# Second feed-forward of a two-layer trunk: Strassen's seven block products in place of eight for the gate and value tiles

## The reference

```
def swiglu(h, w1, w3, w2):
    return (jax.nn.silu(h @ w1) * (h @ w3)) @ w2

x = x + mx[5] * swiglu(modulate(rmsnorm(x, norm_ffn[layer]), mx[3], mx[4]),
                       ffn_w1[layer], ffn_w3[layer], ffn_w2[layer])
```

## Time and profile before

| | |
|---|---|
| median of 3 runs | 2422.42 us (2417.39 to 2422.8) |
| profiled execution | 2426.19 us |
| span of its instructions | 2424.5 us |
| mean granted clock of TensorE | 0.976 of full speed |
| PE busy | 2308.9 us, 95% |
| POOL busy | 1043.5 us, 43% |
| DVE busy | 1402.4 us, 58% |
| ACT busy | 885.7 us, 37% |

### The profile page before, as it was taken

One profiled execution on the slowest core, in us unless ns is written; L12 is line 12 of the kernel. 1 busy time (PEld: TensorE's weight loads), 2 busy tenths in 40 slices (PEclk: granted clock), 3 DMA queues, 4 the chain that ended last, 5 costly groups with the idle time before them and its releaser, 6 DMA issues.

```text
span 2424.5 us, 32675 instructions
## 1 busy us (share of the span) xinstructions
PE 2308.9 (95%) x11883; PEld 1837.2 (76%) x11883; DVE 1402.4 (58%) x1779; ACT 885.7 (37%) x1919; POOL 1043.5 (43%) x815
## 2 busy tenths in 40 slices
PE   6998999999888999999999999999999989999998
PEld 4887888887535888888888887876555557888886
DVE  4997688665677347757766456542567654111113
ACT  4103435433684156746646352232221212201002
POOL 3453243234542434534444434353122125766664
PEclk9999999999988999999999999999999999999999
DMA  8862342354541244434544223454133212333332
GB/s 266 274 184 89 103 129 84 119 181 144 171 121 30 70 69 132 141 110 121 139 116 126 71 76 118 130 165 138 58 110 98 65 44 70 108 94 99 96 97 81
DMA packets 392723, 281.06 MB, mean 116 GB/s; under 512 B 33442, under 2 KB 357820, under 8 KB 392604
## 3 DMA queue, kind: packets, MB, share of 16 engines
q1 hardware_dynamic: 333420, 200.46, 28.8%
q10 hardware_dynamic: 59184, 78.99, 9.6%
HBM read 237.34 MB, written 42.07 MB: 115 GB/s over the span
## 4 chain that ended last, share of the span: by engine, by line
PE 60%; DVE 5%; ACT 2%; issue 1%; ACTq 1%; DMA 1%; POOL 0%; SPq 0%; DVEq 0%; POOLq 0%
PE PS L928 43%; PE PS L1435 4%; PE PS L1606 3%; PE PS L1447 3%; PE PS L1558 2%; PE PS L1526 1%; ACT nh L1711 1%; PE PS L869 1%; PE PS L1507 1%; DVE xcr L2434 1%; ACTq L2102 1%; PE PS L863 0%; PE PS L1384 0%; PE PS L1318 0%; ACT fprod L2053 0%
## 5 line engine op out<-in xcount | busy, mean ns | idle before, releaser
L928 PE MATMUL PS<-act_hi,w_hi 128*128 128x512 f32 (+1 forms) x1824 | 646.0, 354 | 19.6 <-POOL w_lo L738 4.8
L735 POOL TENSOR_TENSOR w_hi<-w_raw,ones 128x128 fp32r<-128x128 f32 x244 | 134.4, 551 | 1210.6 <-DMA w_raw<-in_ffn_w 429.1
L928 PE MATMUL PS<-act_lo,w_hi 128*128 128x512 f32 (+1 forms) x1824 | 637.9, 351 | 0.0
L928 PE MATMUL PS<-act_hi,w_lo 128*128 128x512 f32 (+1 forms) x1824 | 635.3, 348 | 0.0
L738 POOL TENSOR_TENSOR w_lo<-w_raw,w_hi 128x1024 fp32r<-128x1024 f32 (+1 forms) x244 | 588.9, 2414 | 20.3
L928 PEld LDWEIGHTS PS<-act_hi,w_hi 128*128 128x128 f32 x1824 | 347.5, 190 | 77.9 <-issue 14.9
L928 PEld LDWEIGHTS PS<-act_hi,w_lo 128*128 128x128 f32 x1824 | 345.7, 190 | 47.3
L928 PEld LDWEIGHTS PS<-act_lo,w_hi 128*128 128x128 f32 x1824 | 346.8, 190 | 45.5 <-issue 1.2
L2053 ACT ACTIVATE fprod<-mf_ring,cs 128x128 f32<-128x128 f32 x896 | 267.9, 389 | 27.5 <-DVE mf_acc L2349 27.5
L2349 DVE TENSOR_REDUCE mf_acc<-fprod 128x128 f32<-128x1024 f32 x112 | 225.1, 2021 | 89.9 <-ACT fprod L2053 89.9
L736 POOL TENSOR_SCALAR w_hi<-w_raw 128x896 fp32r<-128x896 f32 (+1 forms) x244 | 247.1, 1013 | 0.0
(11 more groups left out here) (364 smaller groups left out, 3588.2 us busy)
## 6 DMA issues: line engine op xcount, KB each, us to landing
w_raw<-in_ffn_w SPq DMA_DIRECT2D x120, 512.0 KB, 4.1
mf_ring<-in_w_mod SPq DMA_DIRECT2D x56, 512.0 KB, 4.0
w_raw<-in_a_w_in SPq DMA_DIRECT2D x44, 512.0 KB, 4.2
proj<-stage ACTq DMA_DIRECT2D x44, 384.0 KB, 3.9
w_raw<-in_b_w_up SPq DMA_DIRECT2D x32, 512.0 KB, 4.7
m_ring<-in_w_mod SPq DMA_DIRECT2D x12, 1024.0 KB, 7.5
rows<-g_d SPq DMA_DIRECT2D x16, 768.0 KB
m_raw<-in_w_mod SPq DMA_DIRECT2D x4, 2048.0 KB, 12.2
```

The costliest lines, as they stand in the source:

```text
L735: pool.tensor_tensor(w_hi[:, s, 0], w_raw[:, s, 0], ones[:], ALU.mult)
L928: last = pe.matmul(to[:, c0:c1], w[:, s, k, :], x[:, k, c0:c1], start=k == 0 and w is w_hi and x is hi, stop=k == kt - 1 and w is w_lo)
```

## The change

The up segments of layer 1 are computed in another way; all else stays. A pair, gate tile G and value tile V, is one product of a 2 x 2 block matrix: output tile (G or V) by feature half (features 0 to 511, 512 to 1023) for the weights, feature half by token half (tokens 0 to 255, 256 to 511) for the activations. Strassen's scheme in Winograd's form makes it of seven products instead of eight, each of 4 feature blocks x 3 passes x 256 columns.

- Weights, per pair: SP loads both raw tiles into `s_raw[q]`, q alternating between two buffers (`load_next`). DVE makes four sums of 128 x 512 elements (`weight_sums`), ACT the high parts of all seven blocks (`weights_high`), POOL the seven low parts (`block_low`), those of the four sums on top of them.
- Activations, once (`norm_blocks`): in four steps of two feature tiles, DVE makes four sums of 256 columns, ACT the high parts of the blocks, DVE their low parts.
- Products (`seven_products`): the seven land in banks 0, 2, 1, 3, 5, 4, 7. A block waits for its low part and for the DVE sums that free its bank. For the first pair of group 0 PE waits for the blocks of two pairs, then takes the seven products a feature block at a time.
- Outputs, per pair: ACT copies the first product (`p1_put`), DVE adds products in seven sums of 256 columns (`parts_of`, `hidden_product`), ACT takes silu of `s_c1`, DVE multiplies it with `s_c2`; the high and low part of the hidden tile as before.
- The buffers `s_hi0`, `s_sum0`, `s_lo0` of q = 0 lie on `w_hi` and `w_raw`. So the first four loads of a down segment wait for the group's last low part and for the last pair but one (SP), and the blocks of the next group's first pair wait for down tiles 4 to 7 (`block_free`). SP no longer loads `w_raw` ahead.
- Before the last two residual tiles of `mout1` DVE makes the weight sums of the first two pairs, ACT their high parts.

```diff
+        s_hi = [nc.alloc_sbuf_tensor_at("s_hi0", [P, BLOCKS, 4, P], F32R, offset=w_hi_at), sb("s_hi1", [P, BLOCKS, 4, P], F32R, offset=61440)]
+        s_lo = [nc.alloc_sbuf_tensor_at(f"s_lo{q}", [P, BLOCKS, 4, P], F32R, offset=(w_raw_at, zst_at)[q]) for q in range(2)]
+        s_sum = [nc.alloc_sbuf_tensor_at(f"s_sum{q}", [P, BLOCKS, 4, P], F32, offset=(w_raw_at, zst_at)[q]) for q in range(2)]
...
+        def block_free(eng, g, r, s, i, first):
+
+            n0 = segs[f"up1{g}"][0]
+            if not first:
+                eng.wait_ge(mm_done, r * RING + (s - 2))
+            elif s == 0:
+                eng.wait_ge(mm_done, n0 - 3 + i // 2)
+            elif g:
+                eng.wait_ge(mm_done, n0 - KD)
...
+                elif name[:5] == "down1":
+                    sp.wait_ge(w_split, n0 + later(name))
+                    for s in range(RING):
+                        sp.wait_ge(mm_done, n0 - 2)
+                        sp.dma_start(w_raw[:, s, 0:kt], src(n0 // RING, s)).then_inc(w_in[s], 16)
+                    each_ring(sp, n0 + RING, count - RING, load)
...
+                        for i in range(BLOCKS):
+                            pool.wait_ge(whi_done, count_at(g, r, e, BLOCKS, WHI0 + i + 1))
+                            if i in (1, 3):
+                                pool.wait_ge(wsum_done, count_at(g, r, e, 4, WSUM0 + (3 if i == 1 else 4)))
+                            x = raw_block(q, i) if i in (0, 5, 6) else s_sum[q][:, i]
+                            pool.tensor_tensor(s_lo[q][:, i], x, s_hi[q][:, i].bitcast(F32), ALU.subtract).then_inc(w_split, 1)
...
+                (hi, lo), to = moving(i, k), product_bank(i)
+                for n, (w, x) in enumerate(((s_hi, hi), (s_hi, lo), (s_lo, hi))):
+                    last = pe.matmul(to, w[q][:, i, k], x, start=k == 0 and n == 0, stop=k == 3 and n == 2)
...
+                    if not first:
+                        if i == 0:
+                            pe.wait_ge(p1_put, count_at(g, r, s, 1, P1_PUT0))
+                        elif i != 2:
+                            pe.wait_ge(part_done, count_at(g, r, s, 7, PART1 - 7 + (0, 4, 4, 4, 5, 6, 7)[i]))
+                    pe.wait_ge(w_split, split_at(g, r, s, i + 1))
+                    block_product(s // 2, i)
...
+            def parts_of(g, r, s, head=False, ahead=True, first=False):
...
+                if not head:
+                    hidden_product(g, *previous(r, s))
+                if ahead:
+                    weight_sums(g, *following(r, s), first)
+                if not head:
+                    hidden_low(g, *previous(r, s))
+                dve.wait_ge(p1_put, count_at(g, r, s, 1, P1_PUT0 + 1))
+                dve.wait_ge(prod_mm, count_at(g, r, s, 6, PROD0 + 4))
+                dve.tensor_tensor(s_u2[:], s_p1[:], product_bank(3), ALU.add).then_inc(part_done, 1)
```

More of the change, by code:

```diff
@@ L727, in _, with split @@
                                      pattern=[[-1, P]], channel_multiplier=1), consts)
[L730 removed]
+            def split(r, s, kt, n0=None, less=0):
                 pool.wait_ge(w_in[s], r * 16 + 16)
[L732 removed]
+                if n0 is not None:
+                    pool.wait_ge(mm_done, n0 - 2)
+                elif not (isinstance(r, int) and r == 0):
                     pool.wait_ge(mm_done, r * RING + (s - RING + 1))
@@ L1671, in root, with weights_high @@
                 rstds[0] += 1
+            def weights_high(g, r, s, blocks, first=False):
+                q, e = s // 2, swapped(g, s, first)
+                for i in blocks:
+                    block_free(act, g, r, s, i, first)
+                    if i in (0, 6):
+                        act.wait_ge(w_in[s + i // 6], r * 16 + 16)
+                    if 1 <= i <= 4:
+                        act.wait_ge(wsum_done, count_at(g, r, e, 4, WSUM0 + (1, 2, 3, 4)[i - 1]))
+                    x = raw_block(q, i) if i in (0, 5, 6) else s_sum[q][:, i]
+                    act.activation(s_hi[q][:, i], x, ACT.Copy).then_inc(whi_done, 1)
             def squares(name, n):
                 g = NORMS.index(name)
+                r1 = segs["up10"][0] // RING
                 for k in range(KD):
+                    if name == "ffn1" and k == KD - 2:
+                        weights_high(0, r1, 2, range(BLOCKS), True)
+                    if name == "ffn1" and k == KD - 1:
+                        weights_high(0, r1, 0, range(BLOCKS - 1), True)
                     act.wait_ge(evac, segs[NORM_AFTER[name]][0] + k + 1)
@@ new lines, in _ @@
+            norm_blocks()
+            for g in range(3):
+                n0, count = segs[f"up1{g}"][:2]
+                r0, r1 = n0 // RING, (n0 + count) // RING - 1
+                if g:
+                    weights_high(g, r0, 0, range(BLOCKS), True)
+                gates_of(g, r0, 0, head=True, ahead=g > 0, first=True)
+                gates_of(g, r0, 2)
+                each_ring(act, n0 + RING, count - 2 * RING, lambda r, s: gates_of(g, r, s))
+                gates_of(g, r1, 0)
+                gates_of(g, r1, 2, ahead=False)
+                hidden_high(g, r1, 2)
@@ new lines, in _ @@
+            norm_blocks()
+            for g in range(3):
+                n0, count = segs[f"up1{g}"][:2]
+                r0, r1 = n0 // RING, (n0 + count) // RING - 1
+                parts_of(g, r0, 0, head=True, ahead=g > 0, first=True)
+                parts_of(g, r0, 2)
+                each_ring(dve, n0 + RING, count - 2 * RING, lambda r, s: parts_of(g, r, s))
+                parts_of(g, r1, 0)
+                parts_of(g, r1, 2, ahead=False)
+                hidden_product(g, r1, 2)
+                hidden_low(g, r1, 2)
+                if g == 2:
+                    residual("down12", 1, 5, LAT, then="final")
+                    continue
+                residual(f"down1{g}", 1, 5, LAT, tiles=range(KD - 1))
+                weight_sums(g + 1, segs[f"up1{g + 1}"][0] // RING, 0, True)
+                residual(f"down1{g}", 1, 5, LAT, tiles=(KD - 1,))
```

248 lines of the change are left out of this document (237 added, 11 removed).

## The result

The changed kernel takes 2475.99 us, median of 4 runs (2473.64 to 2485.57), where the kernel before takes 2422.61 (2417.39 to 2433.95, 4 runs). The ratio is 1.022, 95% interval 1.018 to 1.027: slower by 53 us. The prediction was 2465, range 2430 to 2484. The median of the kernel before moves by some us from one series of runs to the next: the three series of the experiments have 2427.0, 2425.1 and 2426.6 us, and against those the changed kernel, which was not run again, would be 49 to 51 us slower. Of all runs of all kernels one, of psum_operand, took 3649 us at a mean granted clock of 0.576; the time given for that kernel is the median of its other three runs.

What follows compares the result with a forecast made beforehand. The prediction took PE's stream of matmuls to bound the kernel, with DVE and POOL setting the pace after the change. Its terms summed to +42.8 us on the profiled 2426.2 us, given as 2465 us against the median, range 2430 to 2484.

Steps and rivals of the forecast that it cites:

- the forecast case: Layer-1 up stages: DVE and POOL shut each other out, 11.5 us a pair; 2465 us in all, chance 0.47.
- PE's products: Up stages: 84 matmuls of 256 columns a pair replace 96 of 512, 10.04 us instead of 10.88; -18.6 us.
- pace of the pairs: Up stages: DVE and POOL hand-overs make 14 pairs take 11.5 us against PE's 10.04; +20.4 us.
- holes before down: Before each down stage PE idles for a late load and two splits, 9.0, 9.0 and 7.4 us; +25.4 us.
- clock behind idle: After each of three holes before down stages, PE's matmuls run at the lower clock for a while; +5 us.
- norm in front: Norm before the up stages: PE waits for DVE's split blocks, 5.5 us a step for 2.5 of work; +12.6 us.
- sums ahead of it: Before the norm: eight weight sums on DVE delay the last residual tile; +3 us.
- waits that go: Second feed-forward: most of 5.5 us beyond matmuls and transposes are up-stage waits that vanish; -5 us.
- rival (d): Unbroken streams of 256-column matmuls fall to the 0.19 us of a weight load; +130 us, chance 0.01.
- (a): Up stages: DVE and POOL miss each other, pace 10.04 us a pair, short holes; -11 us, 2411 us, chance 0.10.
- (b): Up stages: half of the hand-overs happen, pace 10.9 us, holes of 6, 6 and 5; +24 us, 2446 us, chance 0.24.
- (c): Up stages: POOL itself is the pace, 12.3 us a pair, and last into each down stage; +60 us, 2482 us, chance 0.18.

Runs made afterwards that it cites:

- psum_operand: Changed kernel, but the weight sums of all pairs except each group's first two read one operand from PSUM and compare instead of adding; 2444.36 us.
- all_stage: Changed kernel plus two of seven low parts moved to DVE, earlier first down-stage loads, gate value and hidden product in PSUM; 2432.51 us.
- all_norm: all_stage plus first-pair weight sums moved behind the norm's sum of squares and PE waiting there block by block; 2428.86 us, ratio 1.001.

## Why the prediction was right

The outcome is the forecast case, 11 us above its number; in the profiled executions some 5 of them are in the changed part (+47.6 against +42.8). Part of the closeness is luck: the pace cost 6.0 us more than its term and the holes 5.7 less. What is left over is the clock, 2.9 more, and the waits that did not go, 3. Step by step, for the profiled execution:

| term | predicted | measured | from |
|---|---|---|---|
| PE's products | -18.6 | -19.7 | pairs without waits take 9.98, before 10.88 |
| pace of the pairs | +20.4 | +26.4 | up stages against those of psum_operand, less 3.0 of clock |
| holes before down | +25.4 | +19.7 | 7.65 + 6.24 + 5.84 |
| clock behind idle | +5 | +7.9 | down stages +1.4, +2.0, +1.5; two pairs of 14.3 us, 1.5 each |
| norm in front | +12.6 | +10.4 | spread's end to first pair's end 23.2, before 13.7, and 0.9 of the first term |
| sums ahead of it | +3 | +4.6 | 12.9 against 8.4 |
| waits that go | -5 | -2 | 2.0 in up 0 alone |
| sum | +42.8 | +47.3 | the stages have +47.6 |

- **PE's products.** The pitch is 0.119 for 256 columns in unbroken streams too. 9.98 us a pair are 0.1188 a matmul, so rival (d) is out. The 109 ns that the formula of the Trainium skill gives (TensorE: Matmul & The Clock Gate, "Back-to-back issue gap") don't fit the stream of the changed kernel either. The page gives that formula for an isolated matmul, not for a stream with a weight load for each, which the prediction did not say.
- **The pace.** Mechanism, place and engine were right. 11.5 was 11.70 in the steady pairs: four operations stand at 1.78 (1.71 from start to start), as I had it, but the two that I put at 0.75 took 1.25 (the product, L3337) and 0.92 (the fourth sum, L2877) on average. Once in each group (the last pair of groups 0 and 1, the fourth of group 2) all six are at 1.25 to 1.8 and PE waits 2.6 us. I had no term for it.

```profile
2152.65 0.38 PE L1779 MATMUL PS<-m_hi,s_hi 128*128 128x256 f32 x1 [2.60 <-DVE s_c L3362]
```

- **The holes.** Composition and length right: load and two splits took 12.3 us in the first (2156.39 to 2168.7), as worked out. The start was too late by mine: SP's wait ended 5.0 us ahead of PE's last product (2161.4), 6.6 and 5.0 at the other two holes, not 3.4. The pair in which PE waits 2.6 us may be what gives POOL this time; no run shows it.
- **Clock.** I counted holes only. Waits inside pairs of 2.6 us were followed by the low clock in two of three cases (granted clock 0.5 from 2298.3 to 2301.7 and from 2397.2 to 2400.7, but full behind the wait at 2152.65). Windows behind the first hole (clock is the column after POOL's) show it:

```profile
2169.00:2171.70 2.70, 2.65 (x6) 2.15 (x7) 0.00 (x0) 0.00 (x0) 2.62 (x3) 0.50 0.00 0
2172.00:2210.00 38.00, 38.00 (x164) 30.65 (x164) 4.62 (x7) 0.64 (x1) 20.40 (x17) 1.00 0.40 111
```

- **The norm.** Steps of 4.8 us, not 5.5: DVE's operations start some 0.08 us before the one ahead has ended by its row, and I added rows up. PE's matmuls up to 2073 run at the low clock (0.50), but that costs nothing at the end, since the last step waits for DVE again. PE's waits in it:

```profile
2067.23 0.55 PE L1779 MATMUL PS<-m_hi,s_hi 128*128 128x256 f32 x1 [4.84 <-DVE m_t L3329]
...
2076.75 0.39 PE L1779 MATMUL PS<-m_hi,s_hi 128*128 128x256 f32 x1 [1.59 <-DVE m_t L3329]
...
2080.35 0.39 PE L1779 MATMUL PS<-m_hi,s_hi 128*128 128x256 f32 x1 [0.83 <-DVE m_t L3329]
```

- **What goes.** Wrong: of the 5.5 us only 2.0 lay in up stages. The others were no waits at all: in the down stages the matmuls of 512 columns follow each other every 0.233 us in place of 0.2267, without an idle row, 1.3 us for 192 of them, and that stayed.
- **Rivals.** (a), 2411, would have needed DVE and POOL to miss each other. psum_operand is nearest to that: its weight sums don't meet POOL, no pair waits, and it ends at 2444. Even all_stage, with no waits in two groups and holes of 2.2, 2.1 and 0.2 us, ends at 2432. My 2411 took the lower bound of 8 for all of the norm, where norm and the sums ahead of it are 15 together, and 5 us of waits as gone, where 2 went. (b) needed a pace of 10.9, (c) POOL as the pace, which psum_operand excludes, although its number, 2482, is closer to 2476 than mine. By the number alone (c) would have won; the terms decide for the forecast: a pace of 11.7 and not 12.3, and holes of 20 us and not 30.

The larger part of the result is therefore shown: 29 us of the up stages go with the operands' place alone, 12 (holes) to 15 (stage sum) with the loads' wait, and of the 15 in and ahead of the norm (10.4 + 4.6) 13 remain in the best order that was tried (all_norm: 7.9 + 95.9, less the seven later pairs' 69.9, is 33.9; before 8.4 and 13.7, and 0.9 of the first term is added).
